# Single-head attention with keys first, modulation sums in the feed-forward, and decay sums for two levels by one product

## The reference

```python
# second block, per layer; x are 256 latent tokens, xc 256 context tokens
mod = silu(c) @ w_ada[l] + b_ada[l]        # 1024 -> 3072, once for c and once for c_ctx
h = rmsnorm(x, g_pre) * (1 + scale) + shift
p = split(h @ w_in[l])                      # conv, q, k, v, gates, recurrence
# attention: 8 query heads, 2 key heads of width 128, 512 keys
s = q @ k.T * scale; att = softmax(s) @ v   # q, k normed by row; latents also rotated
# recurrence (4 heads, 128 key and 256 value columns), in both directions
att[t, s] = sum_d q[t, d] * k[s, d] * exp(bcum[t, d] - bcum[s, d])   # s <= t
o = att @ v + (q * exp(bcum)) @ state
```

## Time and profile before

| | us |
|---|---|
| median of 3 runs (lowest, highest) | 2431.46 (2429.3, 2434.36) |
| the profiled execution | 2429.52 |
| its span, first to last instruction | 2427.5 |
| TensorE busy | 2301.8 |
| VectorE busy | 1514.7 |
| ScalarE busy | 971.3 |
| GpSimd busy | 34.1 |

### The profile page before, as it was taken

One profiled execution on the slowest core, in us unless ns is written; L12 is line 12 of the kernel. 1 busy time (PEld: TensorE's weight loads), 2 busy tenths in 40 slices (PEclk: granted clock), 3 DMA queues, 4 the chain that ended last, 5 costly groups with the idle time before them and its releaser, 6 DMA issues.

```text
span 2427.5 us, 34541 instructions
## 1 busy us (share of the span) xinstructions
PE 2301.8 (95%) x13618; PEld 2029.9 (84%) x13618; DVE 1514.7 (62%) x2774; ACT 971.3 (40%) x1533; POOL 34.1 (1%) x37
## 2 busy tenths in 40 slices
PE   7899999999999999999978999999989989889997
PEld 6788888789889899978866888888879889759997
DVE  6879996779995466554354534653465665456665
ACT  5564454565444434332223321222245434234343
POOL 0000000000000000000000000000001000000000
PEclk9899998999998999999978999999999999899999
DMA  5347864347763311123310333333222224305552
GB/s 182 93 158 240 263 204 147 114 132 245 256 213 128 96 44 36 36 71 96 83 31 0 96 96 96 97 96 103 79 79 63 62 63 155 96 9 174 173 183 105
DMA packets 177240, 284.65 MB, mean 117 GB/s; under 512 B 9460, under 2 KB 66932, under 8 KB 176824
## 3 DMA queue, kind: packets, MB, share of 16 engines
q1 hardware_dynamic: 174976, 276.60, 36.7%
q10 hardware_dynamic: 2104, 5.85, 0.7%
HBM read 281.37 MB, written 1.05 MB: 116 GB/s over the span
## 4 chain that ended last, share of the span: by engine, by line
PE 75%; DVE 13%; DVEq 4%; ACT 4%; issue 3%; DMA 1%; ACTq 0%; SPq 0%
PE bank L1858 20%; PE bank L1859 20%; PE bank L1860 20%; DVE WLO L920 3%; PE bank L2063 1%; PE bank L2480 1%; PE bank L2236 1%; PE bank L2235 1%; PE bank L2500 1%; PE bank L2298 1%; DVEq L1336 1%; DMA RAW<-in_e_w_in 1%; DVE ARENA L1333 1%; ACT WHI L464 1%; PE bank L2322 1%
## 5 line engine op out<-in xcount | busy, mean ns | idle before, releaser
L920 DVE TENSOR_TENSOR WLO<-RAW,WHI 128x1024 fp32r<-128x1024 f32 (+2 forms) x500 | 582.4, 1171 | 510.0 <-ACT WHI L464 497.1
L464 ACT ACTIVATE WHI<-RAW 128x1024 fp32r<-128x1024 f32 (+2 forms) x500 | 506.8, 1017 | 904.1 <-PE bank L1860 865.0
L1858 PE MATMUL bank<-ATH,WHI 128*128 128x256 f32 (+1 forms) x2032 | 660.8, 325 | 8.5 <-DVE ARENA L1473 2.1
L1859 PE MATMUL bank<-ATL,WHI 128*128 128x256 f32 (+1 forms) x2032 | 653.9, 322 | 0.0
L1860 PE MATMUL bank<-ATH,WLO 128*128 128x256 f32 (+1 forms) x2032 | 653.8, 322 | 0.0
L1858 PEld LDWEIGHTS bank<-ATH,WHI 128*128 128x128 f32 x2032 | 388.8, 191 | 41.7 <-DVE ARENA L1586 2.3
L1860 PEld LDWEIGHTS bank<-ATH,WLO 128*128 128x128 f32 x2032 | 388.7, 191 | 28.6
L1859 PEld LDWEIGHTS bank<-ATL,WHI 128*128 128x128 f32 x2032 | 388.9, 191 | 28.1
L1858 PE MATMUL bank<-WHI,ATH 128*128 128x512 f32 (+2 forms) x996 | 359.3, 361 | 10.7 <-DVE WLO L920 7.4
L1859 PE MATMUL bank<-WLO,ATH 128*128 128x512 f32 (+2 forms) x996 | 353.5, 355 | 0.0
L1860 PE MATMUL bank<-WHI,ATL 128*128 128x512 f32 (+2 forms) x996 | 353.2, 355 | 0.0
(11 more groups left out here) (284 smaller groups left out, 2567.9 us busy)
## 6 DMA issues: line engine op xcount, KB each, us to landing
RAW<-in_w_in SPq DMA_DIRECT2D x192, 512.0 KB, 3.6
RAW<-in_w_ff SPq DMA_DIRECT2D x128, 512.0 KB, 4.7
ARENA<-in_w_ada SPq DMA_DIRECT2D x64, 384.0 KB, 4.8
RAW<-in_o_w_in SPq DMA_DIRECT2D x24, 512.0 KB, 3.9
RAW<-in_e_w_in SPq DMA_DIRECT2D x16, 512.0 KB, 4.8
RAW<-in_w_ple_gate SPq DMA_DIRECT2D x16, 512.0 KB, 4.1
RAW<-in_w_br_gla SPq DMA_DIRECT2D x16, 512.0 KB, 3.6
RAW<-in_w_br_attn SPq DMA_DIRECT2D x16, 512.0 KB, 3.5
```

What stands on the lines that cost most here:

```text
L464: nc.scalar.activation(WHI[:, slot, 0:n], RAW[:, slot, 0:n], ACT.Copy).then_inc(hi_split, 1)
L920: V.tensor_tensor(WLO[:, slot, 0:n], RAW[:, slot, 0:n], WHI[:, slot, 0:n], ALU.subtract).then_inc(lo_split, 1)
L1858: mm(o, ah, bh, start=start, stop=False, skip_group_check=free)
L1859: mm(o, ah, bl, start=False, stop=False, skip_group_check=free)
```

## The change

Modulation: the sums over partitions of the quarter made in one feed-forward step are put into the next step, after the third slot of its second block of hidden columns, in free columns of bank 3; ScalarE copies these to MOD. Only the last quarter stays where all were. Recurrence: two levels of one tile and direction are summed by one product 256 columns wide; the triangles' columns are stored in the order that this needs, ScalarE sorts while it takes the exponent, and P2 now holds both levels of a pair for all tiles. Orders on TensorE, VectorE and ScalarE are rewritten around it. Attention: the keys are projected first and normed, rotated and scaled while the queries are projected, and the heads run one at a time, each step of one head beside another step of the next.

```diff
@@ weight order
-            (f"q{n}", 2, [std(w, C_Q, BLK)]), (f"k{n}", 1, [std(w, C_K, width=AKV * AD)]),
+            (f"k{n}", 1, [std(w, C_K, width=AKV * AD)]), (f"q{n}", 1, [std(w, C_Q + half * BLK) for half in range(2)]),
@@ ScalarE, feed-forward
+                            if j == 1 and c == 3 and T.i:
+                                nc.scalar.activation(MOD[:, layer, (T.i - 1) * MOD_STEP:T.i * MOD_STEP, :],
+                                                     bank[c][:, S:S + 2 * MOD_STEP].rearrange("p (n v) -> p n v", v=2), ACT.Copy)
@@ ScalarE, decay sums
+                def gla_pair(i, p, *which):
+                    if p:
+                        act.wait_ge(g_level, (layer * GH + i) * (1 + len(LEVELS)) + 2 * p + 1)
+                    for t in which:
+                        if t >= nq:
+                            continue
+                        act.wait_ge(g_diff, T.next(g_diff))
+                        for l in range(2):
+                            dst, src = P2[:, l, t, :, :].rearrange("p k n -> p (k n)"), bank[t % 2][:, l * 2 * P:(l + 1) * 2 * P]
+                            half = LEVELS[2 * p + l]
+                            last = nc.scalar.activation(dst.rearrange("p (m e x) -> p m e x", e=2, x=half),
+                                                        src.rearrange("p (e m x) -> p m e x", e=2, x=half), ACT.Exp)
+                        last.then_inc(g_exp, 1)
+
+                def gla_last(i):
+                    act.wait_ge(g_level, (layer * GH + i) * (1 + len(LEVELS)) + len(LEVELS) - 1)
+                    exps(LASTE[:, 0:tq], bank[0][:, 0:tq])
...
@@ ScalarE, order of one head
                     taken(i, 3)
                     next_hi(i, 3)
-                    gla_level(i, 2)
                     gla_abs()
-                    gla_level(i, 3)
+                    gla_pair(i, 1, 0, 1, 2, 3)
                     gla_logs()
-                    gla_level(i, 4)
                     taken(i + 1, 0)
                     next_hi(i + 1, 0)
-                    gla_level(i, 5)
-                    gla_level(i, 6)
+                    gla_pair(i, 2, 0, 1, 2, 3)
+                    taken(i + 1, 1)
+                    gla_last(i)
                     gla_tiles(0, 1, 2, 3)
-                    taken(i + 1, 1)
+                    gla_pair(i + 1, 0, 0, 1)
                     gla_turned()
-                    gla_level(i + 1, 0)
-                    gla_level(i + 1, 1)
+                    gla_pair(i + 1, 0, 2, 3)
                     taken(i + 1, 2)
                     next_hi(i + 1, 1, 2)
@@ VectorE, modulation
-                V.tensor_tensor(MOD[:, layer, :, :], bank[0][:, 0:6 * KC].rearrange("p (c v) -> p c v", v=2),
-                                b_ada.to_broadcast([P, 3 * KC, 2]), ALU.add).then_inc(bank_free[0], 1)
+                late = (FF_STEPS - 1) * MOD_STEP
+                V.tensor_tensor(MOD[:, layer, 0:late, :], MOD[:, layer, 0:late, :], b_ada[:, 0:late, :].to_broadcast([P, late, 2]), ALU.add)
+                V.tensor_tensor(MOD[:, layer, late:3 * KC, :], bank[0][:, 0:2 * MOD_STEP].rearrange("p (c v) -> p c v", v=2),
+                                b_ada[:, late:3 * KC, :].to_broadcast([P, MOD_STEP, 2]), ALU.add).then_inc(bank_free[0], 1)
@@ VectorE, products of one level
-                    dve.wait_ge(g_exp, T.next(g_exp, nb))
-                    e = P2[:, n % 2, 0:nb, :, :]
-                    V.tensor_tensor(e[:, :, 0, :], e[:, :, 0, :], q.rearrange("p (b n) -> p b n", b=nb), ALU.mult)
-                    V.tensor_tensor(e[:, :, 1, :], e[:, :, 1, :], key.rearrange("p (b n) -> p b n", b=nb), ALU.mult).then_inc(g_pair, 1)
+                    if n % 2 == 0:
+                        dve.wait_ge(g_exp, T.next(g_exp, nq))
+                    for k, x in ((0, q), (1, key)):
+                        e = P2[:, n % 2, 0:nq, k, :]
+                        last = V.tensor_tensor(e, e, x.rearrange("p (t n) -> p t n", n=P), ALU.mult)
+                    last.then_inc(g_pair, 1)
@@ VectorE, order of one head
                     gla_place(0)
+                    gla_min()
                     gla_place(1)
-                    gla_min()
-                    for n in range(2, 5):
-                        gla_level(n, i)
-                        gla_place(n)
+                    gla_place(2)
+                    gla_level(2, i)
+                    gla_level(3, i)
+                    gla_place(3)
+                    gla_place(4)
                     gla_decays(i + 1)
+                    lo(1)
+                    gla_level(4, i)
                     gla_level(5, i)
                     gla_place(5)
-                    lo(1)
+                    gla_place(6)
                     gla_level(6, i)
-                    gla_place(6)
                     gla_place(7)
                     gla_keys(i + 1)
                     gla_squares()
                     gla_roots()
+                    gla_rows()
                     gla_level(0, i + 1)
-                    gla_rows()
                     gla_level(1, i + 1)
                     gla_gains(i)
@@ VectorE, attention (the helper bodies are those of before)
+                drain()
                 V.tensor_scalar(KG, KG, col("k_norm_g_2", layer), None, ALU.mult).then_inc(a_gain, 1)
+                groups(0, query_in)
+                key_scales()
+                base = T.now(gemm_step)
+                lo(SLOTS - 1)
+                keys_done()
+                for c in range(4):
+                    dve.wait_ge(gemm_step, base + 4 * (SLOTS - 1) + c + 1)
+                    query_in(1, c)
+                lo(1)
+                T.next(gemm_step, 4 * SLOTS)
+                drain()
+                base = T.now(gemm_step)
+                lo(1)
+                query_scales()
+                lo(SLOTS - 2)
+                for c in range(TT):
+                    dve.wait_ge(gemm_step, base + TT * (SLOTS - 1) + c + 1)
+                    freed(V.tensor_copy(VA[:, c, :], bank[c][:, 0:AKV * AD]), c)
+                lo(1)
+                T.next(gemm_step, TT * SLOTS)
+                drain()
+
...
+                for n in range(AH + 2):
+                    if n + 1 < AH:
+                        gain(n + 1)
+                    if 1 <= n <= AH:
+                        divide((n - 1) % 2)
+                    if n < AH:
+                        maxima(n)
+                    if n >= 2:
+                        stored(n - 2)
+                    if n + 1 < AH:
+                        rotate((n + 1) % 2)
@@ TensorE, modulation
+                def step_sums(i):
+                    def work():
+                        pe.wait_ge(ada_used, (layer + 1) * ADA_BUFS + (layer * FF_STEPS + i + 1) * 2 * SLOTS)
+                        for n in range(MOD_STEP):
+                            for v in range(2):
+                                at = (i * MOD_STEP + n) * P
+                                mm(bank[3][:, S + 2 * n + v:S + 2 * n + v + 1], ACC[v][:, at:at + P], cst("ones")[:, 0:1],
+                                   start=False, stop=False, skip_group_check=True)
+                    return work
+
+                pe.wait_ge(const_in, 16)
                 for i in range(FF_STEPS):
                     cols_block(first, after={0: turn_second} if i == 0 else {})
-                    cols_block(first)
+                    cols_block(first, after={2: step_sums(i - 1)} if i else {})
                     if i == 0:
-                    for n in range(3 * KC):
-                        last = mm(bank[0][:, 2 * n + v:2 * n + v + 1], ACC[v][:, n * P:(n + 1) * P], cst("ones")[:, 0:1], start=True, stop=True)
+                    for n in range(MOD_STEP):
+                        at = ((FF_STEPS - 1) * MOD_STEP + n) * P
+                        last = mm(bank[0][:, 2 * n + v:2 * n + v + 1], ACC[v][:, at:at + P], cst("ones")[:, 0:1], start=True, stop=True)
@@ TensorE, decay sums
+                def gla_pair(i, p, *which):
+                    for t in which:
+                        if t >= nq:
+                            continue
+                        exps_done(i, 4 + p * nq + t - 1)
+                        for d in range(2):
+                            at0 = TRI_LEVEL + (2 * p + d) * 2 * P
+                            columns = TRI[:, at0:at0 + 2 * P].rearrange("p (l k n) -> p l k n", l=2, k=2)
+                            whole, first, apart = bank[t % 2][:, :], P // 2 * (1 - d), P // 2 * (1 + 2 * d)
+                            o = bass.AP(whole.tensor, whole.offset + first, [list(whole.ap[0]), [2 * P, 2], [apart, 2], [1, P // 2]])
+                            last = gla_sums(i, o, d, t, columns)
                         last.then_inc(g_diff, 1)
@@ TensorE, order of one head
                     gla_outer(i)
                     columns(i, 3, 1)
-                    gla_inter()
+                    gla_inter(i)
                     gla_scores(0, i)
-                    gla_scores(1, i)
+                    gla_pair(i, 1, 0, 1)
```

(37 more changed lines are left out.)

380 lines of the change are left out of this document (174 added, 206 removed).

## The result

The changed kernel takes 2370.6 us (median of four runs, 2367.5 to 2376.5) against 2430.4 us before (2426.8 to 2434.4): a ratio of 0.9749, 95% interval 0.9733 to 0.9765. The forecast was 2366 us with a range of 2350 to 2398. The profiled execution's span is 2366.5 us, 61.0 us less than before.

What follows compares the result with a forecast made beforehand. TensorE was taken as the main bound (75% of the chain of waits, VectorE 13%). Gains of 8 + 33 + 11 + 13 = 65 us off the profiled 2429.5 gave 2364.5, predicted as a 2366 us median; range 2350 to 2398.

Steps and rivals of the forecast that it cites:

- Half of the eight rows: Modulation: half of the eight parts of 24 sums lower the clock, leaving 8 us of a possible 14.3.
- moving them saves nothing by itself: Modulation: all 96 sums per layer cost 10.6 us wherever they stand, so only the clock pays.
- the gate's weights: Modulation: wanted 11 us sooner, the gate's weights are just covered, or cost up to 1 us if not.
- what hides it: Modulation: what is added elsewhere is covered, such as ScalarE's copy of 12 columns and TensorE's wait for the quarter.
- The term of 29 us for the instructions: Recurrence: half as many sums, twice as wide, save 4.8 and 2.4 us per head, four heads each.
- The waits: Recurrence: waits grow about 0.6 us per first-layer head, gain 4.2; the last layer's head takes 36.8 us, gain 4.5.
- The new wait: Attention: TensorE waits 5.8 us from v's end for VectorE's head 0 rotation, two splits and four v copies.
- the queries' sums: Attention, first layer: 64 instructions, some 42 at 0.11 and 22 at 0.21 us, 9.2 us, plus 1.5 for slow products.
- The clock: Rival: every part of 24 sums and attention's gap per head lower the clock; gain 51, 2380 us; chance 0.14.
- The single-buffered P2: Rival, recurrence: each handover some 2.1 us late, three per head; total gain 28, 2403 us; chance 0.11.
- Wide sums: Rival, recurrence: 256-column sums take 0.22 us, so it yields 4 instead of 33; 2395 us; chance 0.04.
- Single heads: Rival, attention: heads run in series, 15.3 us each in the first layer; 2441 us, slower than before; chance 0.03.

Runs made afterwards that it cites:

- the row of 72: Kernel after the change, with the modulation sums of each feed-forward's first three steps in one row in its last step: 2378.4 us, 0.9773.
- the experiment: Kernel after the change, with ScalarE waiting for and squaring the context rows behind the second layer's third gate weight split, VectorE's roots later too: 2366.0 us, 0.9729.
- the narrow sums: Kernel after the change, with each 256-column recurrence sum made as two products of 128 columns, same orders and waits: 2399.8 us, 0.9870.
- the tail experiment: Kernel after the change, with a column half back between scores 7 and values in the recurrence's last head, level 6 before VectorE's weight split: 2366.0 us, 0.9722.
- v's copies set first: Kernel after the change, with VectorE copying v's four tiles before rotating head 0 and splitting v's next weights while v is made: 2360.7 us, 0.9703.
- the kernel with all four edits: Kernel after the change plus v's copies ahead of rotation, later context squares, queries' sums of squares in two parts, and the last head's tail reordered: 2344.6 us, 0.9631.

## Why the prediction was right, step by step

**Modulation** (8 us forecast, 7.9 in the traces, 9 alone). A row of 24 costs 2.6 us, as said, and what splitting saves on the instructions is what the clock costs, which the row of 72 shows. Half of the eight rows were taken to lower the clock; it is three in the kernel after and 42 of 80 over the ten executions. The 192 sums take 20.9 us instead of 32.5, and the slow products behind them 4.6 instead of 3.6: 10.6 us by the clock. That the total is 7.9 all the same is luck, since waits that the sum did not have go both ways. The kernel before has two waits in each layer between the feed-forward and the sums (timeline of TensorE before the change, first layer):

```profile
344.42 1.09 PE L1923 MATMUL bank<-CST,h 128*128 128x128 f32 x8 [1.05 <-DVEq L1352]
...
354.97 1.09 PE L1923 MATMUL bank<-CST,h 128*128 128x128 f32 x8 [0.49 <-DVEq L1352]
```

They are gone in every kernel with the sums in the feed-forward, the one with that part alone included, and stand in the two without it: 3.1 us gained for both layers. So "moving them saves nothing by itself" was wrong. The two waits were for VectorE's addition to h (L1352); the likely reason that they went is that VectorE is nearly full in that stage, and has caught up by the time TensorE has made the sums as well (busy 136.55 us in the window from 190 to 340 us instead of 141.59). Against that, a bank that was free again by the end of 96 sums is awaited for 0.5 us behind 24, in both layers.
The larger loss is a wait in the second layer. The prediction bounded the gate's weights by 1 us for the first gate alone; in the second layer ScalarE waits 7.3 us for the context's rows ahead of its splits, and before the change the 17 us of sums covered that. The wait on TensorE is 2.9 us, and with the slow products behind it 3.4 us came back in the experiment. The step that failed is "what hides it": the queue of the engine that feeds the weights was not followed past the sums in the second layer.
The Trainium skill ("TensorE: Matmul & The Clock Gate", HAM oscillation) warns of lulls in which TensorE waits, again and again; the prediction read it as speaking against scattered rows, with a gain of 2. TensorE does not wait in these rows. The clock did fall behind about half of them, at 1.4 to 3.1 us each, but a row of 72 costs more than three of 24, and the gain was 8 us.

**Recurrence** (33 us forecast, 32.9). The term of 29 us for the instructions is what the narrow sums gave back by the medians, 27 in the recurrence's own stages. The waits were judged too high in the first layer and too low in the last: heads 51.0 and 37.5 us instead of 52 and 36.8. The rest lies at the ends of the stage. Its start gave 8.6 us in the first layer (19.5 to 10.9), with 1.6 us of a wait for ScalarE and 2.3 us of slow products gone. About 3.4 of it is part of the 4.8 us that the sum has for a head: level 2's sums now stand inside each head and no longer ahead of it, so of the last head's saving only some 1.4 us are left for its tail. That tail did not gain even this, but lost 2.1 us in the first layer and 0.1 in the last. A column half had been moved from ahead of scores 7 to behind the values, and TensorE waits 2.6 us there. This is the second missed wait, and the tail experiment shows it. Here too the start and the tail cancel, and 32.9 against 33 is in part luck.

**Attention up to the first scores** (11 us, 10.1). The new wait was put at 5.8 us from v's end to the scores, and is 5.8 in both layers; its cause, VectorE standing in the rotation while v ends, is shown by v's copies set first. The terms given for the first layer add up to 21.3 us and not 21.1. The mis-sized term is the queries' sums: 11.2 us instead of 9.2 in the first layer, and 2.3 us of slow products behind instead of 1.5. The last layer gained 2 more than forecast ahead of attention: the first 192 products of the branch take 25.5 us instead of 28.1, at a granted clock of 1.00 instead of 0.89. The kernel with the recurrence's part alone has the 25.5 too, so this gain belongs to the recurrence, where a wait of 3.4 us just ahead of these products went.

**Heads** (13 us, 9.9). In the steady state a head takes 8.46 and 5.80 us against 8.5 and 6.0 forecast, and the window from 1231 to 1281 us, which holds the steady part alone, reads full clock:

```profile
1211.00:1231.00 20.00, 15.73 (x46) 9.65 (x47) 11.12 (x29) 6.91 (x19) 0.00 (x0) 0.76 0.20 65
1231.00:1281.00 50.00, 41.73 (x202) 31.41 (x200) 32.74 (x90) 25.09 (x66) 0.00 (x0) 1.00 0.00 0
```

What was mis-sized is the start: with the pauses of 5.2 and 2.8 us ahead of the first two heads' scores the clock is 0.76 over this stretch. In the last layer, where 4.1 of 5 us came, the same code takes 52.9 us in three of the other kernels and 54.3 and 56.7 in two, so that miss is within what one trace can tell.

**The rivals.** The clock fell behind about half of the rows of 24 and not in the steady heads. The single-buffered P2 does not bind: the scores wait 0.43 us per head in the first layer (the price given for it adds up to 2.3 us, not 2.1, which changes nothing), and the exponents of 256 columns cost the 0.3 us that were taken (four in 1.21 us). Wide sums do not stream slower. Single heads overlap, with no wait over 1.3 us once under way and up to 1.7 us behind the last two.

## What to carry to other kernels

Where a full TensorE runs small products, count instructions and not columns: twice the width for half the number was worth nearly its whole instruction time here (4.8 us of 4.8 per head in the first layer, 2.1 of 2.4 in the last). One-column fp32 products belong in short rows between dense ones; what that saves on them is the clock, and the waits around their old place change as well, in both directions. When a long stretch of TensorE time is taken away, follow each feeding engine's queue through that stretch in every layer: both large waits that were missed (2.9 and 2.6 us) were things that the old order had covered. And compare a forecast part by part and layer by layer: a total that fits can be a sum of errors.

## What had not been expected of the hardware

A row of one-column products lowers the clock although TensorE does not pause in it, and the fall may come behind the row, on innocent products: with 32 instructions (3.5 us at full speed) it did in all 11 rows of the runs, in both layers, with 16 (1.7 us) in none of 34, with 24 (2.6 us) in 42 of 80, and the place counts: the first row of the second layer fell ten times in ten, the two rows that a short wait follows always, the last row in the second layer's feed-forward never. Why the first row of a layer is the likely one was not settled. With a pause of 5.2 us ahead of them the first layer's first scores take 5.3 us; with a pause of 1.7 us they take 2.7. But the length of a pause alone does not decide. The second head's scores, behind the same pause of 3.1 us, run at half speed with v's copies first (3.49 us for four) and at full speed in the kernel with all four edits (timeline of TensorE):

```profile
1206.78 1.98 PE L2566 MATMUL bank<-ARENA 128*128 128x512 f32 x4 [3.09 <-DVE ARENA L1731]
```

Near this place the two kernels differ in the queries' sums, one row of 64 or two of 32. Whether that is the cause was not tested.
